# A decoder layer's top-k selection: counts spread over the band steps in rotation, a fourth tile counted early on ScalarE, and the index scores moved to later projection halves

## The reference

```python
rel = relu(einsum('bthd,bsd->bths', iq, ik))
score = einsum('bths,bth->bts', rel, iw) * idx_scale      # 8 index heads, summed with weights
score = where(causal, score, -inf)
_, sel = lax.top_k(score, 256)                            # per query; then softmax attention over sel
```

## Time and profile before

| | |
|---|---|
| median of three runs | 1642.15 us (1636.99 to 1645.26) |
| the profiled execution | 1636.79 us, of which span 1635.0 us |
| PE busy | 1523.3 us (93%) |
| DVE busy | 898.7 us (55%) |
| ACT busy | 466.7 us (29%) |
| POOL busy | 554.9 us (34%) |
| mean granted TensorE clock | 0.967 |

### The profile page before, as it was taken

The page is one execution under the profiler, slowest core; times in us unless marked ns, Lnnn a source line. Parts: engine busy times, 40 slices in busy tenths (PEclk is TensorE's granted clock), DMA queues, the critical chain, the costliest instruction groups (busy, mean ns, idle before and its releaser), DMA issues.

```text
span 1635.0 us, 20812 instructions
## 1 busy us (share of the span) xinstructions
PE 1523.3 (93%) x7720; PEld 1294.8 (79%) x7720; DVE 898.7 (55%) x1819; ACT 466.7 (29%) x987; POOL 554.9 (34%) x554
## 2 busy tenths in 40 slices
PE   7998887788978999999999999999999999999996
PEld 7876666788867997778887788888888888888884
DVE  7577887688897433593426733333333333333357
ACT  3124456888444651121210211111111111111010
POOL 5240356556630003341233153333333333333300
PEclk9998998999977999999999999999999999999998
DMA  5435242643710004211110221111111110111001
GB/s 224 155 129 155 78 168 104 193 144 100 241 59 14 14 1 174 92 45 52 52 52 0 78 77 52 52 52 52 52 52 52 52 52 27 52 52 52 1 26 78
DMA packets 61332, 128.97 MB, mean 79 GB/s; under 512 B 6960, under 2 KB 34096, under 8 KB 53552
## 3 DMA queue, kind: packets, MB, share of 16 engines
q1 hardware_dynamic: 44208, 100.37, 18.2%
q10 hardware_dynamic: 17024, 27.27, 4.7%
HBM read 100.35 MB, written 27.26 MB: 78 GB/s over the span
## 4 chain that ended last, share of the span: by engine, by line
PE 72%; DVE 16%; issue 4%; ACT 3%; DMA 2%; POOL 1%; SPq 1%; ACTq 0%; DVEq 0%; POOLq 0%
PE banks L699 21%; PE banks L701 21%; PE banks L700 21%; PE banks L898 3%; DVE unread L1533 2%; PE banks L753 2%; PE banks L754 2%; PE banks L885 2%; ACT unread_wide L1098 1%; PE banks L907 1%; DVE h_buf L1859 1%; DVE bn L1845 1%; DVE score L1500 1%; DVE h_buf L1868 1%; PE banks L854 1%
## 5 line engine op out<-in xcount | busy, mean ns | idle before, releaser
L685 POOL TENSOR_SCALAR w_hi<-raw 128x512 fp32r<-128x512 f32 x268 | 174.2, 676 | 890.5 <-PE banks L701 652.9
L690 POOL TENSOR_TENSOR w_lo<-raw,w_hi 128x512 fp32r<-128x512 f32 x268 | 365.3, 1395 | 0.0
L1959 DVE TENSOR_TENSOR h_buf<-h_buf,banks 128x1024 f32<-128x1024 f32 x112 | 136.8, 1221 | 145.8 <-PE banks L701 145.8
L699 PE MATMUL banks<-act_hi,w_hi 128*128 128x512 f32 x512 | 199.4, 389 | 1.7 <-DVE act_lo L1838 1.7
L699 PE MATMUL banks<-w_hi,hid_hi 128*128 128x512 f32 x512 | 199.3, 389 | 1.4 <-DVE hid_lo L1939 1.4
L700 PE MATMUL banks<-w_lo,hid_hi 128*128 128x512 f32 x512 | 199.2, 389 | 0.0
L701 PE MATMUL banks<-act_hi,w_lo 128*128 128x512 f32 x512 | 199.2, 389 | 0.0
L700 PE MATMUL banks<-act_lo,w_hi 128*128 128x512 f32 x512 | 199.2, 389 | 0.0
L701 PE MATMUL banks<-w_hi,hid_lo 128*128 128x512 f32 x512 | 199.2, 389 | 0.0
L1324 ACT ACTIVATE relu_buf<-banks 128x512 f32<-128x512 f32 x64 | 38.3, 599 | 521.5 <-PE banks L701 521.5
L1934 DVE TENSOR_TENSOR relu_buf<-relu_buf 128x512 f32<-128x512 f32 x64 | 45.3, 708 | 239.8 <-ACT relu_buf L1324 239.8
(11 more groups left out here) (177 smaller groups left out, 2826.1 us busy)
## 6 DMA issues: line engine op xcount, KB each, us to landing
raw<-w_up_dram SPq DMA_DIRECT2D x16, 1024.0 KB, 4.8
raw<-w_down_dram SPq DMA_DIRECT2D x16, 1024.0 KB, 4.8
q_tile<-qk_dram SPq DMA_DIRECT2D x176, 64.0 KB, 2.3
qk_dram<-q_hi ACTq DMA_DIRECT2D x28, 256.0 KB, 2.1
qk_dram<-roped ACTq DMA_DIRECT2D x28, 256.0 KB, 2.3
x_raw<-x_t_dram SPq DMA_DIRECT2D x8, 512.0 KB, 8.2
raw<-wk_mem_dram SPq DMA_DIRECT2D x4, 1024.0 KB, 5.0
raw<-wv_mem_dram SPq DMA_DIRECT2D x4, 1024.0 KB, 5.7
```

The costliest lines, as they stand in the source:

```text
L685: pool.tensor_scalar(w_hi[s][:, col], raw[c % 2][:, col], 1.0, 1.0, ALU.mult, ALU.mult)\
L690: pool.tensor_tensor(w_lo[s][:, col], raw[c % 2][:, col], w_hi[s][:, col].bitcast(F32), ALU.subtract).then_inc(w_ready, 1)
L699: pe.matmul(dst, lh, rh, start=(first and n == 0), stop=False)
L1959: dve.tensor_tensor(h_buf[:, t, :], h_buf[:, t, :], ring_l[n % 2][:], ALU.add)\
```

## The change

The index scores of tiles 7, 6, 5, 4, 2, 3 now stand in halves 15 to 20 (before: tiles 2 and 3 in 10 and 11, tiles 7, 6, 5, 4 in 14 to 17), so counting begins at half 21, not 18, and no queries are loaded before the last index unit is stored. Beside halves 21 to 27 ACT counts four tiles (7, 6, 5 and now 4) for seven bits, 28 counts. In the band steps it counts the remaining 24 bits of tiles 7, 6, 5: 72 counts, in rotation, two or three to a step over steps 3 to 31, the first of a step before the memory moves, the others at its end. Tile 4 goes back to DVE after its seventh bit (`take_over`), which counts tiles 2, 3, 4 in one loop, with one `find` for all three, and finishes tile 4 with the wide ones. The discarded output of the late counts lies elsewhere, so SP waits only for the 28 early ones.

```diff
-INDEX_HALVES = {10: 2, 11: 3, 14: 7, 15: 6, 16: 5, 17: 4}
+INDEX_HALVES = {15: 7, 16: 6, 17: 5, 18: 4, 19: 2, 20: 3}
-N_INDEX_FIRST = 2
+N_INDEX_FIRST = 0
...
-COUNT_STEP = {WIDE_SPAN * j // WIDE_LEFT: TOP_BIT - N_EARLY - j for j in range(WIDE_LEFT)}
...
+COUNTS = [(c, TOP_BIT - j) for j in range(N_EARLY) for c in EARLY_TILES]
+N_EARLY_COUNTS = len(COUNTS)
+COUNTS += [(c, k) for k in range(LAST_EARLY_BIT - 1, -1, -1) for c in WIDE_TILES]
+COUNT_FROM, COUNT_TO = 3, 32
...
+def counts_at(n):
+
+    if not COUNT_FROM <= n < COUNT_TO:
+        return range(0)
+    left = len(COUNTS) - N_EARLY_COUNTS
+    lo, hi = (left * (m - COUNT_FROM) // (COUNT_TO - COUNT_FROM) for m in (n, n + 1))
+    return range(N_EARLY_COUNTS + lo, N_EARLY_COUNTS + hi)
...
+                if c == C_MEM + 4:
+
+                    sp.wait_ge(wide_counted, N_EARLY_COUNTS)
                     load_key(0, dsa_keys_in)
...
+                for q in counts_at(n)[0:1]:
+                    count_scores(q)
                 for use in products_at(n)[0:1]:
                     move_memory(use)
...
-                if wide_bit_counted(n) is not None:
-                    count_wide(wide_bit_counted(n))
+                for q in counts_at(n)[1:]:
+                    count_scores(q)
...
+                def bisect(n, bits):
+
+                    for k in bits:
+                        for c in range(n):
+                            cost, counted = narrow_tally(c)
+                            yield cost + 0.25, None
+                        dve.wait_ge(dve_step, counted)
+                        dve.wait_ge(dve_step, then(dve.tensor_scalar(refused[:, 0:n], count[:, 0:n], 0.0, float(1 << k),
+                                                                     ALU.is_lt, ALU.mult)))
+                        for c in range(n):
+                            set_at[c] = then(set_next(c, k))
...
-                yield from bisect((0, 1))
-                yield from bisect_alone(2, finish_narrow((0, 1)))
-                yield from finish_narrow((2,))
+                yield from bisect(EARLY, range(TOP_BIT, LAST_EARLY_BIT - 1, -1))
+                take_over(EARLY)
+                yield from bisect(WIDE, range(LAST_EARLY_BIT - 1, -1, -1))
+                yield from finish_narrow((0, 1))
```

More of the change, by code:

```diff
@@ L1137, in _ @@
                         round_mem()
-                    if wide_bit_beside_rope(v) is not None:
-                        count_wide(wide_bit_beside_rope(v))
+                    for q in counts_beside_rope(v):
+                        count_scores(q)
                     for n in index_own(v):
@@ L1567, in narrow_tally, with take_over @@
                     return tally(c, ALU.is_ge, trial[:, c:c + 1].bitcast(F32), minus_rank[:, c:c + 1]), written[-1]
-                def narrow_set(c, k, counted):
-                    dve.wait_ge(dve_step, counted)
-                    dve.wait_ge(dve_step, then(find_refused(c, k, 0.0)))
-                    set_at[c] = then(set_next(c, k))
-                def bisect(cols):
-                    waiting = None
-                    for k in range(top, -1, -1):
-                        for c in cols:
-                            cost, counted = narrow_tally(c)
-                            if waiting is not None:
-                                narrow_set(*waiting)
-                            waiting = (c, k, counted)
-                            yield cost + 0.3, None
-                    narrow_set(*waiting)
-                def bisect_alone(c, beside):
-                    for k in range(top, -1, -1):
-                        cost, counted = narrow_tally(c)
-                        yield cost + 0.3, None
-                        more = next(beside, None)
-                        if more is not None:
-                            yield more
-                        narrow_set(c, k, counted)
-                    yield from beside
+                def bisect(n, bits):
+                    for k in bits:
+                        for c in range(n):
+                            cost, counted = narrow_tally(c)
+                            yield cost + 0.25, None
[4 more added lines that the diff above has]
+                            set_at[c] = then(set_next(c, k))
+                def take_over(c):
+                    assert early_set[0]
+                    dve.wait_ge(trial_ready, len(EARLY_TILES) + N_EARLY_COUNTS)
+                    set_at[c] = then(dve.tensor_scalar(trial[:, c:c + 1], trial[:, c:c + 1], SIGN_BIT, None,
+                                                       ALU.bitwise_xor))
                 def finish_narrow(cols):
@@ L1653, in select_keys @@
                 chain(dve.tensor_tensor(threshold[:, wide], sign[:, wide], level[:, wide], ALU.mult))
-                for c in range(WIDE, N_SEL):
+                for c in range(EARLY, N_SEL):
                     yield from finish(c)
@@ L1658, in _, with set_counted, find, apply @@
             wide_set = [False]
-            def set_wide(k):
-                def find(m, c):
-                    dve.wait_ge(wide_counted, (TOP_BIT - k) * N_WIDE + m + 1)
-                    found_at[c] = then(find_refused(c, k, offset[:, c:c + 1]))
-                def apply(m, c):
-                    dve.wait_ge(dve_step, found_at[c])
-                    set_next(c, k).then_inc(trial_ready, 1)
-                    if k == 0 and m == N_WIDE - 1:
-                        wide_set[0] = True
-                found_at = {}
-                steps_of = []
-                for m, c in enumerate(WIDE_TILES):
-                    steps_of += [lambda m=m, c=c: find(m, c), lambda m=m, c=c: apply(m, c)]
-                return steps_of
+            early_set = [False]
+            def set_counted(q):
+                c, k = COUNTS[q]
+                at = []
+                def find():
+                    dve.wait_ge(wide_counted, q + 1)
+                    at.append(then(find_refused(c, k, offset[:, c:c + 1])))
+                def apply():
+                    dve.wait_ge(dve_step, at[0])
+                    set_next(c, k).then_inc(trial_ready, 1)
+                    early_set[0] |= q == N_EARLY_COUNTS - 1
+                    wide_set[0] |= q == len(COUNTS) - 1
+                return [find, apply]
+            def set_all(counts):
+                for q in counts:
+                    pending.extend(set_counted(q))
             selection = select_keys()
```

71 lines of the change are left out of this document (36 added, 35 removed).

## The result

Changed kernel: 1631.68 us median (1629.89 to 1632.76, 6 runs); the kernel before, beside it, 1641.15 us (1636.99 to 1645.26, 6 runs). Ratio 0.9941, 95% interval 0.9921 to 0.9961. So it is faster by 0.6%, 9.5 us; 1630 was forecast.

What follows compares the result with a forecast made beforehand. PE, busy 93% of the span, was taken as the bound, so only its pauses could give time. Terms -8.4 - 7.5 + 3 + 1 = -11.9 took 1642.15 to 1630 us; range 1618 to 1648.

Steps and rivals of the forecast that it cites:

- Projections: Half 10 to the end of half 27: 155.3 us in place of 163.75, -8.4, from -17 to +4.
- The block: Index halves 15 to 20: 64.3 us of heads, 15 of pauses, 4 for half clock, sum 83.3.
- The 4 us for half clock: Index halves 15 to 20: half of the 8.8 us that the old four index halves lost to half clock.
- a price for every pause: Index halves: by the skill's rule, as many pauses lose 8.8 us to half clock, not 4; the projections give -3.6.
- Steps 0 to 2: Nine counts leave; masks 0 and 1, last rotation, mask 2, two tallies follow: -7.5 us, between 0 and -8.
- Steps 3 to 31: ACT's 72 counts: 157.5 us against 154.5, +3; the first count's trial is set a whole step earlier.
- the ring: Band steps: ACT's first count waits for DVE's trial while DVE waits for ACT's last count; 185 us, +30.5.
- rival C: Steps 3 to 31: ACT becomes the slower wall, 1658 us; decides from a mean step of 6.0 us; chance 0.12.
- The bound of 185 us: Upper end for steps 3 to 31: ACT's 150 us at 81%, from 41.5 of 51.28 us in steps 3 to 11.
- Two of the signs: Steps 3 to 31: they take 154 to 161 us, and ACT is over 90% occupied in them.
- Steps 32 to 52: Seven tile 4 bits go, finishing of tiles 2 and 3 comes: +1 us, -2 to +5; step 39 some 2 longer.
- Rival D: DVE's selection is the chain: gains before step 40 go to waits for masks, 2 us remain, 1640; chance 0.07.

Runs made afterwards that it cites:

- e2: Changed kernel with the first count of a step moved to the step's end with the others: 1625.50 us, 0.9914 of the kernel before.
- e11: Changed kernel with DVE's budget of narrow work per band step 2.4 in place of 1.8: 1628.30 us, 0.9924 of the kernel before.
- e1: Changed kernel with its joint find replaced by two or three finds of one column: 1628.05 us, 0.9922 of the kernel before.
- e6: Changed kernel with single finds and all counts at the end of a step: 1624.76 us, 0.9901 of the kernel before.
- e3: Kernel before with only the index scores moved to halves 15 to 20: 1639.44 us, 0.9987 of the kernel before.
- e4: Changed kernel with the index scores back in halves 10, 11 and 14 to 17: 1629.34 us, 0.9921 of the kernel before.
- e5: Changed kernel without ACT's early counts of tile 4, which DVE counts from the first bit: 1634.10 us, 0.9954 of the kernel before.
- e7: Changed kernel with single finds, counts at a step's end and index scores in the old halves: 1622.58 us, 0.9883 of the kernel before.

## Why the prediction was right, and where it was not

**Projections, -8.4 forecast, -7.6 measured from half 10 to mask 0.** The parts held nearly, and their sum better than they did. Halves 10 to 14 took 27.2 us (90.23 to 117.44), as forecast. The block took 81.25 against 83.3: PE was busy for 66.2 us (64.3 forecast) and stood still for 15.0 (15 forecast). The 4 us for half clock were none there. They came in the next halves: in 21 to 26 PE was busy for 36.6 us, at a clock of 0.92, where six plain halves are 32.6. The pairs of halves 23 and 24, and 25 and 26, took 15.1 and 14.9 us (14 to 15 was forecast), and halves 21 to 27 46.5 where 44.8 was forecast. Half 27 started at 239.71, so that half 10 to the end of half 27 is 154.9, forecast 155.3: that this is so near is luck, one miss against another. The halves 21 to 26 had 0.92 in e2 and e11 as well. The index block did not repeat: the same code showed 83.42 and 86.44 us in e2 and e11, with PE busy for 4.4 and 7.4 us longer than here, so this term goes from 0 to over 5 from one execution to the next. The Trainium skill ("TensorE: Matmul & The Clock Gate", HAM oscillation — how this bites in real kernels) tells of a kernel that is throttled anew at each of its long waits. The prediction made of that a price for every pause, 8.8 us in all, and the trace does not bear this out: five pauses of 2.1 to 2.8 us stood in the block, and its clock was 1.00 here, 0.94 and 0.90 in the other two executions.

**Steps 0 to 2, -7.5 forecast, -7.5 measured** (16.34 to 8.84), with the order of work that was named.

**Steps 3 to 31, +3 forecast, +7.7 measured.** This term was mis-sized. The load was judged well: with the ring opened the stretch takes 155.8 to 157.3 us (e1, e2, e6), and 157.5 had been forecast. The step that failed is its reason, that the first count "is due from a trial set a whole step earlier" and so costs no wait. The trial was set late: 13.6 us of waits, up from 4.2. It is the ring of rival C at a sixth of its price (162.2 less e6's 157.1, where 30.5 was named): 5.59 us a step, below the 6.0 from which it was to decide. The bound of 185 us held far too much, and its 41.5 of 51.28 us is in no row: the earlier trace rows have ACT busy for 43.13 us in steps 3 to 11, 84%, which makes 178. Two of the signs missed: 162.2 lies above the 154 to 161 given, and ACT was occupied for 89% of the stretch (133.8 busy and 10.0 in waits for its own moves), not over 90. Part of the lateness was DVE's joint find, which the prediction had counted as a relief ("some 60 finds fewer"); it cost 15.2 us for 20, against 5.3 for 59 single ones.

**Steps 32 to 52, +1 forecast, -1.1 measured.** Step 39 grew by 3.9 us, not 2: tile 2's finishing stands ahead of the first mask as forecast (8.18 us, DVE busy 7.80). The steps before it, 32 to 38, were 5.2 shorter, which the prediction did not have: 4.7 us of PE's work fell ahead of mask 32, as shown above, so it belongs with the 7.7 of steps 3 to 31. From mask 3 to mask 53 the forecast was +4 and the result +6.5; in e6, with the ring opened, it is +1.0. Why PE's work came earlier was not tried; e3, which has only the index halves of the change, does not show it (932 matmuls in steps 3 to 31). Rival D's claim, that DVE's work up to step 52 is what counts, is right of the kernel but did not decide this change: 50.98 and 51.06 us.

**The rest** of the profile, +1.7 us behind mask 53 and +0.3 ahead of half 10, is the same work in both; 1.4 of it lies in masks 53 to 87, at a clock of 0.97 against 0.99. The sum is -7.61 - 7.50 + 7.66 - 1.14 + 1.71 + 0.28 = -6.6, the difference of the spans. The medians are 9.5 apart, since the profiled execution of before was as fast as its fastest other run, 4.4 below the median beside it, and that of the changed kernel 1.5 below its own. So the terms add up to -11.9 in the forecast and to -6.6 in the traces, and a part of how near 1630 came to 1631.68 is in how these two executions lie.

**What the sum hid.** It was right as a sum over stretches, and wrong as a reason. The forecast's largest term, the index move, is real where it was looked for (12.1 us alone, 11.3 between e4 and the changed kernel), but it moves bits of all tiles out of the projections, and beside e4 the changed kernel pays 7.2 us in steps 3 to 31 and 10.7 in 39 to 52 for it, with 6.1 back in 32 to 38. The gain of the kernel comes from the other half of the change, the counts spread out and tile 4's early counts: e4 has them alone, and is as fast. The parts of that half were not all taken apart: the steps 0 to 2 are the spread's (7.1 to 8.0 us, in every kernel that has it), and in the new halves tile 4's early counts are worth some 2 us by e5, which is within the uncertainty; what SP's earlier wait gives was not tried alone. The ring costs 5.1 us in steps 3 to 31 of the new halves (162.2 to e6's 157.1), and 8.8 in the old ones (e4's 155.0 to e7's 146.2, with ACT's waits for a trial down from 11.7 to 1.6), so e4 too had it.

## What to carry to other kernels

When work is moved from one stage to an earlier start of another, price the work that it displaces, in the stage where that lands: time here went from the projections to the last bits of the selection, one for one. Look for rings, in which two engines wait for each other (13.6 and 13.8 us here), before taking either for the bound. The wait that tells is the one on the engine with the most to do: ACT's fell from 13.6 to 1.1 us as the ring was opened, DVE's rose to 23.2. One edit at either side opened it, and the second gave nothing more. Fewer VectorE instructions are not less VectorE time when the merged one can be held up by GpSimd.
